# Inverse roots of the normalisations by bit-level guess and three Newton steps on VectorE

## What is computed

```python
def layer_norm(x, g, b):
    mu = jnp.mean(xf, axis=-1, keepdims=True)
    var = jnp.mean(jnp.square(xf - mu), axis=-1, keepdims=True)
    y = (xf - mu) * lax.rsqrt(var + LN_EPS) * g + b

def rms_norm(u, g):
    y = uf * lax.rsqrt(jnp.mean(uf * uf, axis=-1, keepdims=True) + EPS)
    return y * g
```

## Time and profile before

| | us |
|---|---|
| median of 3 runs (2476.28 to 2477.47) | 2476.84 |
| the profiled execution | 2474.57 |
| its span in the profile | 2473.2 |
| PE busy (97% of the span) | 2411.4 |
| DVE busy (61%) | 1500.7 |
| ACT busy (45%) | 1109.0 |

### The profile page before, as it was taken

One profiled execution on the slowest core, in us unless ns is written; L12 is line 12 of the kernel. 1 busy time (PEld: TensorE's weight loads), 2 busy tenths in 40 slices (PEclk: granted clock), 3 DMA queues, 4 the chain that ended last, 5 costly groups with the idle time before them and its releaser, 6 DMA issues.

```text
span 2473.2 us, 28654 instructions
## 1 busy us (share of the span) xinstructions
PE 2411.4 (97%) x11302; PEld 1992.0 (81%) x11302; DVE 1500.7 (61%) x2117; ACT 1109.0 (45%) x1388; POOL 0.2 (0%) x4
## 2 busy tenths in 40 slices
PE   8999999999999999999999997898999999999999
PEld 7888888888888888888788776687888888888887
DVE  4565999865544555577567576476655555554443
ACT  4444444544444444454446454344544444443333
POOL 0000000000000000000000000000000000000000
PEclk9999999999999999999999998899999999999999
DMA  7645666656665776575545443253566666666664
GB/s 266 193 156 168 194 189 194 213 179 213 195 195 155 255 228 192 181 229 182 166 152 175 161 144 131 88 169 117 187 188 189 187 191 191 187 191 192 201 201 143
DMA packets 124227, 452.99 MB, mean 183 GB/s; under 512 B 13691, under 2 KB 15916, under 8 KB 123068
## 3 DMA queue, kind: packets, MB, share of 16 engines
q1 hardware_dynamic: 124092, 451.17, 58.3%
HBM read 448.99 MB, written 2.12 MB: 182 GB/s over the span
## 4 chain that ended last, share of the span: by engine, by line
PE 95%; DVE 3%; ACT 1%; DMA 1%; issue 0%; SPq 0%; ACTq 0%; DVEq 0%
PE ps L453 88%; PE ps L325 1%; DVE t_wlo L394 1%; PE ps L585 1%; PE ps L535 1%; ACT t_whi L393 1%; PE ps L1399 1%; PE ps L568 1%; PE ps L499 0%; PE ps L975 0%; PE ps L1521 0%; DMA t_raw<-w_out 0%; PE ps L434 0%; DVE t_st L472 0%; DMA t_raw<-w_kv 0%
## 5 line engine op out<-in xcount | busy, mean ns | idle before, releaser
L453 PE MATMUL ps<-t_whi,t_A 128*128 128x512 f32 (+1 forms) x4992 | 1554.0, 393 | 27.0 <-DVE t_wlo L394 12.9
L394 DVE TENSOR_TENSOR t_wlo<-t_raw,t_whi 128x1024 fp32r<-128x1024 f32 x805 | 980.6, 1224 | 873.7 <-ACT t_whi L393 868.0
L393 ACT ACTIVATE t_whi<-t_raw 128x1024 fp32r<-128x1024 f32 x805 | 849.0, 1058 | 1120.6 <-PE ps L453 1107.8
L453 PEld LDWEIGHTS ps<-t_whi,t_A 128*128 128x128 f32 x4992 | 929.5, 189 | 219.1 <-DVE t_wlo L394 14.3
L453 PE MATMUL ps<-t_wlo,t_A 128*128 128x512 f32 (+1 forms) x2496 | 973.6, 390 | 0.0
L453 PEld LDWEIGHTS ps<-t_wlo,t_A 128*128 128x128 f32 x2496 | 471.2, 189 | 98.7
L453 PE MATMUL ps<-t_whi,t_Y0a 128*128 128x512 f32 x1152 | 356.0, 390 | 0.0
L453 PEld LDWEIGHTS ps<-t_whi,t_Y0a 128*128 128x128 f32 x1152 | 215.2, 188 | 44.3 <-DVE t_wlo L394 0.3
L453 PE MATMUL ps<-t_wlo,t_Y0a 128*128 128x512 f32 x576 | 224.3, 389 | 0.0
L453 PEld LDWEIGHTS ps<-t_wlo,t_Y0a 128*128 128x128 f32 x576 | 108.1, 188 | 22.6
L869 DVE SCALAR_TENSOR_TENSOR t_Y1a<-t_H,t_pp,t_Y1a 128x255 f32<-128x255 f32 (+29 forms) x240 | 96.2, 463 | 0.0
(11 more groups left out here) (291 smaller groups left out, 1101.0 us busy)
## 6 DMA issues: line engine op xcount, KB each, us to landing
t_raw<-w_in SPq DMA_DIRECT2D x376, 512.0 KB, 4.1
t_raw<-w_gu SPq DMA_DIRECT2D x176, 512.0 KB, 3.6
t_raw<-w_down SPq DMA_DIRECT2D x88, 512.0 KB, 4.2
t_raw<-w_branch SPq DMA_DIRECT2D x64, 512.0 KB, 4.2
t_raw<-w_out SPq DMA_DIRECT2D x64, 512.0 KB, 3.7
t_raw<-w_ck SPq DMA_DIRECT2D x16, 512.0 KB, 3.6
t_raw<-w_cv SPq DMA_DIRECT2D x16, 512.0 KB, 4.4
t_raw<-w_cq SPq DMA_DIRECT2D x8, 512.0 KB, 3.6
```

Of the source, the lines that this page charges most:

```text
L393: a = S.do(lambda e: e.activation(whi[:, s, 0:n], raw[:, d % NR, 0:n], ACT.Copy), tok, free)
L394: b = V.do(lambda e: e.tensor_tensor(wlo[:, s, 0:n], raw[:, d % NR, 0:n], whi[:, s, 0:n].bitcast(F32), ALU.subtract), a, free)
L453: fn = lambda e, x=x, w=w, kt=kt, k=k, t=t, j=j, bk=bk: e.matmul(bk[:, 0:n], x[:, u["k0"] + kt, t * P:(t + 1) * P], w[:, k, :], start=(kt ...
```

## The change

Where flags["conv"] is set, the inverse root is computed on DVE alone: the bits of the value are shifted right by one and inverted, read as a float and scaled by a constant, which gives a first guess; then three Newton steps of three instructions each. That is eleven instructions on an array of 2 to 16 columns, in place of ACT's root and DVE's reciprocal. Scratch are the conv_w columns of t_pp. inverse_rms() always takes the new way; root() does once the flag is set.

```diff
@@ -7,6 +7,7 @@
 
 F32 = mybir.dt.float32
 F32R = mybir.dt.float32r
+I32 = mybir.dt.int32
 ALU = mybir.AluOpType
 ACT = mybir.ActivationFunctionType
 AX = mybir.AxisListType.X
@@ -23,6 +24,7 @@
 BRANCH = 1024
 NEG = -1e30
 AHEAD = 4.0
+GUESS = 1.835257741510155e-20
 COLS = [range(0, 4), range(4, 9), range(9, 16)]
 SLOPES = [2.0 ** -(h + 1) for h in range(8)]
 
@@ -471,8 +473,7 @@
         c.v(lambda e: e.tensor_tensor(scratch, x, x, ALU.mult), after=after, n=n)
         c.v(lambda e: e.tensor_reduce(r3, scratch, AX, ALU.add), n=n)
         c.v(lambda e: e.tensor_scalar(r, r, 1.0 / width, RMS_EPS, ALU.mult, ALU.add), n=8)
-        c.s(lambda e: e.activation(r, r, ACT.Sqrt), n=1800)
-        return c.v(lambda e: e.reciprocal(r, r), n=8)
+        return inverse_root(c, r)
 
     def norm(c, x, scratch, after=None, extra=None):
 
@@ -488,8 +489,27 @@
     def root(c, r, eps):
 
         c.v(lambda e: e.tensor_scalar(r, r, eps, None, ALU.add), n=8)
+        if flags.get("conv"):
+            return inverse_root(c, r)
         c.s(lambda e: e.activation(r, r, ACT.Sqrt), n=1800)
         return c.v(lambda e: e.reciprocal(r, r), n=8)
+
+    def inverse_root(c, r):
+
+        assert flags.get("conv")
+        rows, n = r.shape
+        y, q = par("conv_w", 0, n)[0:rows, :], par("conv_w", 16, 16 + n)[0:rows, :]
+        steps = [lambda e: e.tensor_scalar(y.bitcast(I32), r.bitcast(I32), 1, 0x7fffffff, ALU.logical_shift_right,
+                                           ALU.bitwise_xor),
+                 lambda e: e.tensor_scalar(y, y, GUESS, None, ALU.mult)]
+        for i in range(3):
+            steps += [lambda e: e.tensor_tensor(q, y, y, ALU.mult),
+                      lambda e: e.scalar_tensor_tensor(out=q, in0=q, scalar=-0.5, in1=r, op0=ALU.mult, op1=ALU.mult),
+                      lambda e, i=i: e.scalar_tensor_tensor(out=r if i == 2 else y, in0=q, scalar=1.5, in1=y,
+                                                            op0=ALU.add, op1=ALU.mult)]
+        for fn in steps:
+            c.v(fn)
+        return c.tok
 
     def turn_start_in_place(c, buf, col, tok):
         b = c.bank()
```

## The result

The changed kernel takes 2493.05 us (2492.27 to 2495.39), the kernel before beside it 2476.61: a ratio of 1.0069, 95% interval 1.0056 to 1.0081, 17 us slower. 2478.6 had been forecast, and the range ended at 2487.

The account below looks back on a forecast made before the run. TensorE, busy 2411.4 of 2473.2 us, was taken as the bound, with only 61.8 us idle to win. Site terms summed to +1.8 us, giving 2478.6 against the median; range 2472 to 2487.

Parts of the forecast that it names:

- the sum of the sites: Effects on PE added over the norms' places: −1.7 −0.45 +0.7 +0.8 +1.65 +0.8 = +1.8 us.
- The steps' length: On DVE, dependent steps start 0.20 us apart; eleven take 2.2 us, net 1.74 per call, 28 us in all.
- Loads counted at nothing: 15 ACT table loads go, 19 us of ACT, valued at zero because they fill time ACT waits anyway.
- Heads 0 and 1: GLA heads 0 and 1: PE's waits on copy L1387 shrink, −1.7 us at head 0 and −0.45 at head 1.
- the other nine: Memory, layer norm, row statistics, slice keys, heads 2 and 3, memory keys: zero; up to 1.74 us each without cover.
- the compressed keys: Compressed keys at 1462 us, with window keys: half of 1.74 us reaches PE, +0.8 (bounds 0 and 1.74).
- The upper bound of +6.4: The costed sites' upper bounds taken together, in us against the forecast sum of +1.8.
- Rival B: Planner's written order shifts, V.now 2.3 us later per call; NSA output's turn 7 us later: 2485.6 us, 32%.
- Its mark: Rival B's sign: PE's wait ahead of the NSA output's L325 turns grows beyond 5 us, or new waits appear.
- The argument against it: Against rival B: with PE idle, the planner forces steps, and the chain runs without chunks in between.
- Rival A: ACT's queue is the bound: heads 0 and 1 and cross-attention free PE, −7.7 us, 2469.1 us, 15%.
- C: Roots stay on ACT except for the two early calls; time stays at 2476.8 us, 2%.

Follow-up runs that it names:

- root_new_order: Kernel before's ACT root and DVE reciprocal, planner's clocks set as for eleven Newton instructions, so PE's order is the changed kernel's: ratio 1.0013, 3.2 us over before.
- newton_old_order: Changed kernel's Newton instructions, planner's clocks set as for root and reciprocal, so the order is the kernel before's: ratio 1.0016, 4.0 us over before.
- root_newton_head2: Changed kernel's order, Newton at GLA head 2 alone, ACT's root at the other 15 norms: ratio 1.0027, 6.7 us over the kernel before.

## Why the prediction was wrong

The step that failed is the sum of the sites: it took each place's cover from the order of the kernel before and put nine places at zero. In that order the sum was not far off (4.0 us against 1.8 forecast, inside the range); in the order that the change itself makes, the same instructions cost 13.9 and the order 3.2.

- **The steps' length: right.** 0.20 us from start to start (0.21 with 16 columns), the integer step no dearer. DVE's busy time rose by 24.8 us (25 forecast), ACT's fell by 26.6 (22 forecast; 20 table loads went, not 15). The Trainium skill (VectorE: DVE Perf Modes, The TRN2 errata) puts the measured fixed part of an operation on SBUF at about 150 cycles of 0.96 GHz, an estimate of 0.16 us; the trace agrees, with 0.16 to 0.17.
- **Loads counted at nothing: not contradicted.** The 15 loads went, and with them five more that the working did not count (two at L1293, one each at L1215, L1477 and L1756): ACT has 36 instructions less, 16 roots and 20 loads. ACT's wait of 31.7 us went too. Newton's price in before's order is +4.0, so no gain is seen. The loads alone were not tried.
- **The sum of the sites in before's order: the sign right, 3.1 too small by the traces.** Heads 0 and 1 came out near what was put down (−2.4 for −2.15), but at head 0 that is luck: PE's 1.71 us went, 2.40 came for DVE's products (L1336), and a later 3.09 went. The failed term there is "zero" for the layer norm among "the other nine": 1.7. Of the 1.74 at the compressed keys I let half arrive; nearly all did.
- **"The other nine … Zero" at heads 2 and 3: the step that cost most.** The working took the cover that the earlier trace rows showed in before's order. In the new order it was gone (6 weight matmuls left instead of 102), and they cost 5.7 us with ACT's root around them and 10 with Newton around them, more than the "up to 1.74" each: a wait passes on to ACT's queue, a delay brought along adds to it, and PE's clock falls behind it. The upper bound of +6.4 left these nine out altogether; at their own 1.74 each they would have added 15.7, and no chance was given to that.
- **Rival B: the right mechanism, its size wrong.** Its mark came true in substance: PE's wait on the low halves (L313) in the NSA output's turn passed 5 us, 1.44 in the earlier trace rows and 5.77 after, at the weights' matmuls L455 and not ahead of the turns. As root_new_order shows, 4.55 of it needs no Newton. B was given 7 us on 14 us of plan and 32%. The order's own price is 3.2; its greater effect, that it takes away the cover under Newton's own steps (10 us more), was not in the working. The argument against it, that the planner forces steps when PE is idle, did not keep the cover; whether it held the order's own price down to 3.2 was not tried.
- **Rival A** is excluded: it lay 7.7 us under before, and newton_old_order, where nothing but the instructions changed, is not faster. **C** is excluded by the trace: no root of the 16 is left on ACT.

## What to carry to other kernels

Where the order is made from estimates, a change of instructions is two changes: price them apart, by setting the planner's clocks by hand, before any site is costed. Cover read from the old trace holds only in the old order; how much is left in the new one can be counted in PE's order, and here it went first in a stage in which PE idled already. And what the planner is told is a knob of its own: here, telling 0 for a root's 0.56 gave 6 us with no instruction changed.

## What the runs showed of the hardware

- PE's clock is a second price on a wait: of the 17.8 us between the profiled executions 8.3 are PE's own busy time with the same number of matmuls, at 0.81 instead of 0.85 in the worst hundred.
- One program's time varies by 0.3% and more with that clock: root_newton_head2 took 2477.5 us at a mean granted clock of 0.991 and 2485.5 at 0.987, so differences under some 4 us needed many runs, and one trace is no measure of its kernel.
